# Down-projection of a two-block layer: two plain pieces ahead of the seven products, and two of the four weight sums made by accumulating transfers

## What is computed

```python
def swiglu(h, w_gate_up, w_down):
    gu = jnp.einsum('bsd,df->bsf', h, w_gate_up)
    gate, up = jnp.split(gu, [FFN_HIDDEN], axis=-1)
    return jnp.einsum('bsf,fd->bsd', jax.nn.silu(gate) * up, w_down)
...
    f = (jax.nn.gelu(g, approximate=True) * u) @ w_down[l]
```

## Time and profile before

| | |
|---|---|
| median of 3 runs | 2674.47 us |
| the profiled execution | 2673.37 us |
| its span, first to last instruction | 2671.6 us |
| TensorE busy | 2640.9 us, 99% |
| DVE, ACT, POOL busy | 1856.3, 1303.7, 3.5 us (69%, 49%, 0%) |
| mean granted clock of TensorE | 0.999 of full speed |
| HBM traffic | 497 MB, mean 186 GB/s |

### The profile page before, as it was taken

The page is one execution under the profiler, slowest core; times in us unless marked ns, Lnnn a source line. Parts: engine busy times, 40 slices in busy tenths (PEclk is TensorE's granted clock), DMA queues, the critical chain, the costliest instruction groups (busy, mean ns, idle before and its releaser), DMA issues.

```text
span 2671.6 us, 37118 instructions
## 1 busy us (share of the span) xinstructions
PE 2640.9 (99%) x13950; PEld 2272.8 (85%) x13950; DVE 1856.3 (69%) x1881; ACT 1303.7 (49%) x1313; POOL 3.5 (0%) x8
## 2 busy tenths in 40 slices
PE   9999999999999999999999999999999999999998
PEld 8888888888888888888888788888888888888877
DVE  7646666665555556875558768888777787677877
ACT  6544444444445444444445556645554454444444
POOL 0000000000000000000000000000000000000000
PEclk9999999999999999999999999999999999999999
DMA  7555555455555555555554554543555546555553
GB/s 250 189 189 174 174 187 188 173 190 190 218 191 179 189 188 206 198 204 184 189 188 162 191 194 172 178 151 133 199 173 188 188 161 217 194 188 189 186 211 134
DMA packets 71871, 497.23 MB, mean 186 GB/s; under 512 B 8183, under 2 KB 9432, under 8 KB 12648
## 3 DMA queue, kind: packets, MB, share of 16 engines
q1 hardware_dynamic: 71784, 496.06, 52.9%
HBM read 493.93 MB, written 2.10 MB: 186 GB/s over the span
## 4 chain that ended last, share of the span: by engine, by line
PE 93%; DVE 4%; ACT 1%; issue 1%; DMA 1%; DVEq 0%; SPq 0%; ACTq 0%
PE acc L2261 37%; PE acc L2269 19%; PE acc L2317 10%; PE acc L2493 7%; PE acc L2324 5%; PE acc L2498 3%; PE acc L2342 2%; DVE w_lo L1285 2%; PE acc L2338 2%; PE acc L2336 2%; PE acc L2365 1%; ACT w_hi L735 1%; PE acc L2620 1%; PE acc L2372 1%; PE aux L2761 1%
## 5 line engine op out<-in xcount | busy, mean ns | idle before, releaser
L1285 DVE TENSOR_TENSOR w_lo<-raw,w_hi 128x2048 fp32r<-128x2048 f32 (+1 forms) x467 | 1063.0, 2280 | 342.7 <-ACT w_hi L735 315.4
L735 ACT ACTIVATE w_hi<-raw 128x2048 fp32r<-128x2048 f32 (+1 forms) x467 | 889.4, 1906 | 801.6 <-PE acc L2261 337.2
L2261 PE MATMUL acc<-xa,w_hi 128*128 128x512 f32 x4480 | 1071.4, 391 | 0.2 <-ACT w_hi L735 0.2
L2261 PEld LDWEIGHTS acc<-xa,w_hi 128*128 128x128 f32 x4480 | 824.3, 188 | 161.8 <-issue 1.1
L2269 PEld LDWEIGHTS acc<-xa,w_lo 128*128 128x128 f32 x4480 | 574.1, 191 | 23.6 <-DVE w_lo L1285 2.0
L2269 PE MATMUL acc<-xa,w_lo 128*128 128x256 f32 x4480 | 581.6, 283 | 1.2 <-DVE w_lo L1285 1.2
L1297 DVE TENSOR_TENSOR tmp<-acc,small 128x512 f32<-128x512 f32 x120 | 82.9, 691 | 234.9 <-ACT small L745 234.4
L2317 PE MATMUL acc<-w_hi,hid 128*128 128x512 f32 x768 | 182.6, 390 | 0.0
L2493 PE MATMUL acc<-w_hi,xa 128*128 128x512 f32 x768 | 182.3, 390 | 0.0
L2317 PEld LDWEIGHTS acc<-w_hi,hid 128*128 128x128 f32 x768 | 143.8, 188 | 29.8
L2493 PEld LDWEIGHTS acc<-w_hi,xa 128*128 128x128 f32 x768 | 143.8, 188 | 29.7
(11 more groups left out here) (379 smaller groups left out, 2097.9 us busy)
## 6 DMA issues: line engine op xcount, KB each, us to landing
raw<-in_w_in SPq DMA_DIRECT2D x158, 1024.0 KB, 4.9
raw<-in_w_gate_up SPq DMA_DIRECT2D x88, 1024.0 KB, 4.9
raw<-in_w_down SPq DMA_DIRECT2D x88, 1024.0 KB, 4.9
raw<-in_w_up SPq DMA_DIRECT2D x87, 1024.0 KB, 4.9
raw<-in_w_out SPq DMA_DIRECT2D x32, 1024.0 KB, 4.9
raw<-in_w_uq SPq DMA_DIRECT2D x3, 1024.0 KB, 4.9
h_tok<-in_x_tok SPq DMA_DIRECT2D x1, 2048.0 KB, 9.3
raw<-in_w_ukv SPq DMA_DIRECT2D x4, 512.0 KB, 3.5
```

The costliest lines, as they stand in the source:

```text
L735: act.activation(hi_part(u, run)[:, 0:kt * P], raw_of(u)[:, 0:kt * P], ACT.Copy).then_inc(hi_made, splits(u, run))
L1285: dve.tensor_tensor(lo_part(u, run)[:, 0:kt * P], raw_of(u)[:, 0:kt * P], hi_part(u, run)[:, 0:kt * P], ALU.subtract).then_inc(lo_made, sp ...
L2261: last = pe.matmul(acc[:, bnk], w_hi[:, u % SPLIT, k * P:(k + 1) * P], x[:, k0 + k], start=first and k == 0, stop=False)
```

## The change

1. The order of a pass is now PLAIN_1, PLAIN_2, M_1, M_5, M_2, PLAIN_3, M_6, M_3, M_7, MIXED, PLAIN_4, M_4, PLAIN_5, PLAIN_6. PLAIN_2's piece is the fifth load of a pass and lies in the slot of PLAIN_1.
2. DVE makes two sums of a pass instead of four: w_sum = B_12 - B_11 as before, and at the end B_21 = B_21 - w_sum. The two between are transfers issued by POOL that add B_22, read once more from HBM, to the slot of B_12 (for M_7) and to w_sum (for M_6). The second waits for M_5's low part, which reads w_sum, and for the first transfer.
3. B_12 + B_22 takes the place of B_22 - B_12, so `hidden_sums` changes signs; it has the same instructions.
4. `weight_sum(u, 1)` moves: in the last `gated` from behind the split of the first piece to behind that of the second; between two passes from PLAIN_5 to PLAIN_6, behind the two additions of `added`.
5. Steps at the ends (squares, transposes, gains) are hung on other forms, as the old ones have moved.

```diff
-PLAIN_1, M_1, M_5, M_2, PLAIN_2, M_6, M_3, M_7, PLAIN_3, M_4, MIXED, PLAIN_4, PLAIN_5, PLAIN_6 = range(FORMS)
+PLAIN_1, PLAIN_2, M_1, M_5, M_2, PLAIN_3, M_6, M_3, M_7, MIXED, PLAIN_4, M_4, PLAIN_5, PLAIN_6 = range(FORMS)
...
     (3, ((0, 1), (1, 1), (2, 1), (3, 1))),
+    (0, ((12, 0), (13, 0), (14, 0), (15, 0))),
     (0, ((4, 0), (5, 0), (6, 0), (7, 0))),
-    (1, ((12, 0), (13, 0), (14, 0), (15, 0))),
...
-FREED_BY = (None, None, None, None, PLAIN_1, M_1, PLAIN_2, M_3, M_7, PLAIN_3, M_4)
-NEXT_SLOTS = (2, 3, 1, 0)
+FREED_BY = (None, None, None, None, PLAIN_1, PLAIN_2, M_1, PLAIN_3, M_3, M_7, M_4)
+NEXT_SLOTS = (1, 2, 3, 0)
...
                 if u in WEIGHT_SUMS:
                     act.wait_ge(w_summed, WEIGHT_SUMS[u])
+                elif u in ADDED_SUMS:
+                    act.wait_ge(w_added, ADDED_SUMS[u])
...
+            def down_sums(start, name):
+
+
+                for n, u in enumerate(s for s in PASS_STARTS if start <= s < start + GROUPS * FF_UNITS):
+                    b_22 = d[name][n // PASSES, n % PASSES, B_22]
+                    pool.wait_ge(w_summed, sums_before(u) + 1)
+                    pool.dma_start(raw[:, PIECE_RAW[u, B_12][0]], b_22, accum_op=ALU.add).then_inc(w_added, 16)
+                    pool.wait_ge(lo_made, u + M_5 + 1)
+                    pool.wait_ge(w_added, 16 * (sums_before(u) + 1))
+                    pool.dma_start(w_sum[:], b_22, accum_op=ALU.add).then_inc(w_added, 16)
+
+            down_sums(U_FF1, "w_down")
             pool.wait_ge(folded, 3)
...
                     out_, a, b = w_sum[:], piece(u, B_12), piece(u, B_11)
                 if n == 2:
-                    dve.wait_ge(lo_made, u + M_5 + 1)
-                    piece_loaded(u, B_22)
-                    out_, a, b = w_sum[:], piece(u, B_22), w_sum[:]
-                if n == 3:
-                    out_, a, b = piece(u, B_12), piece(u, B_22), piece(u, B_12)
-                if n == 4:
                     dve.wait_ge(lo_made, u + M_2 + 1)
-                    dve.wait_ge(w_summed, sums_before(u) + 2)
+                    dve.wait_ge(w_added, 16 * (sums_before(u) + 2))
                     out_, a, b = piece(u, B_21), piece(u, B_21), w_sum[:]
...
-                for m, (out_, a, b, op) in enumerate(((x_22, x_21, x_22, ALU.add), (x_21, x_11, x_21, ALU.subtract),
-                                                      (x_11, x_22, x_11, ALU.subtract), (x_12, x_12, x_11, ALU.subtract))):
+                for m, (out_, a, b, op) in enumerate(((x_22, x_21, x_22, ALU.subtract), (x_21, x_21, x_11, ALU.subtract),
+                                                      (x_11, x_11, x_22, ALU.subtract), (x_12, x_12, x_11, ALU.subtract))):
...
                             split(u + 2, run)
-                        if last and p:
-                            weight_sum(u0 + 2 * GT, 1)
                         total(t, run, 2)
                         dve.tensor_tensor(tmp[:, 0:2], tmp[:, 0:2], rstd2, ALU.mult).then_inc(gate_in, 1)
                         if p or ahead < 2:
                             split(u + 3, run)
+                        if last and p:
+                            weight_sum(u0 + 2 * GT, 1)
...
-                        if form == PLAIN_5 and p + 1 < PASSES:
+                        if form == PLAIN_6 and p + 1 < PASSES:
                             weight_sum(u + FORMS, 1)
```

More of the change, by code:

```diff
@@ L161 @@
     (3, ((0, 1), (1, 1), (2, 1), (3, 1))),
[1 row of a table added]
     (0, ((4, 0), (5, 0), (6, 0), (7, 0))),
[1 row of a table removed]
     (1, ((16, 0), (17, 0), (18, 0), (19, 0))),
[3 rows of a table removed]
[3 rows of a table added]
     (0, ((16, 1), (17, 1), (18, 1), (19, 1))),
 )
-B_11, B_22, B_12, B_21 = 1, 2, 3, 4
-PIECE_OF = {PLAIN_1: 0, M_1: B_11, M_2: B_21, M_3: B_22, PLAIN_2: 5, PLAIN_3: 6, MIXED: 7, PLAIN_4: 8, PLAIN_5: 9, PLAIN_6: 10,
+B_11, B_22, B_12, B_21 = 1, 2, 3, 5
+PIECE_OF = {PLAIN_1: 0, M_1: B_11, M_2: B_21, M_3: B_22, PLAIN_2: 4, PLAIN_3: 6, MIXED: 7, PLAIN_4: 8, PLAIN_5: 9, PLAIN_6: 10,
             M_7: B_12, M_4: B_21}
-FREED_BY = (None, None, None, None, PLAIN_1, M_1, PLAIN_2, M_3, M_7, PLAIN_3, M_4)
-NEXT_SLOTS = (2, 3, 1, 0)
+FREED_BY = (None, None, None, None, PLAIN_1, PLAIN_2, M_1, PLAIN_3, M_3, M_7, M_4)
+NEXT_SLOTS = (1, 2, 3, 0)
 def raw_places():
@@ L552, in sums_before @@
         def sums_before(u):
[L555 to L558 removed]
+            return 2 * PASS_STARTS.index(u)
+        WEIGHT_SUMS = {s + form: sums_before(s) + n for s in PASS_STARTS for form, n in ((M_5, 1), (M_4, 2))}
+        ADDED_SUMS = {s + form: 16 * (sums_before(s) + n) for s in PASS_STARTS for form, n in ((M_7, 1), (M_6, 2))}
         def next_unit(u, run):
@@ L1250, in _ @@
                             act.sem_inc(small_made, 2 * COLS)
-                        if g and p and form == PLAIN_2:
+                        if g and p and form == M_7:
                             out_square(1, 0)
@@ L2206, in _ @@
                             snap(u, b_22, M_7, ff_out[:, 2 * p, 1])
-                        if form == MIXED:
+                        if form == M_7:
+                            weight_sum(u, 2)
+                        if form == M_4:
                             if g:
@@ L2222, in _ @@
                             snap(u, b_12, M_5, ff_out[:, 2 * p + 1, 1])
-                        if form == M_2:
-                            weight_sum(u, 3)
-                        if form == M_3:
-                            weight_sum(u, 4)
-                        if form == PLAIN_5 and p + 1 < PASSES:
+                        if form == PLAIN_6 and p + 1 < PASSES:
                             weight_sum(u + FORMS, 1)
-                        if g and p and form == PLAIN_3:
+                        if g and p and form == MIXED:
                             out_gain(1, 0)
@@ L2390, in down @@
                 plain(PLAIN_1, b_11, 8, first=True)
+                plain(PLAIN_2, b_11, 12)
                 pe.wait_ge(acc_free, b_22 + 1)
@@ L2395, in down @@
                 product(u + M_2, b_11, *hidden(4, 0))
-                plain(PLAIN_2, b_11, 12)
+                plain(PLAIN_3, b_11, 16)
                 pe.wait_ge(snapped, snaps + 1)
@@ L2402, in down @@
                 product(u + M_7, b_22, *hidden(0, 1), final=True, more=True)
-                plain(PLAIN_3, b_11, 16)
-                product(u + M_4, b_21, *hidden(4, 1))
                 if p == 0:
                     pe.wait_ge(op_lo, v1 + GT)
-                pe.wait_ge(snapped, snaps + 4)
-                both_columns(u + MIXED, t)
+                both_columns(u + MIXED, t, snaps + 4)
+                if after:
+                    after(MIXED)
                 plain(PLAIN_4, b_12, 8)
+                product(u + M_4, b_21, *hidden(4, 1), final=True)
                 if not staggered:
```

61 lines of the change are left out of this document (31 added, 30 removed), and 6 rows, old and new, of the table PIECES.

## The result

The changed kernel takes 2716.27 us (median of 4 runs, 2708.99 to 2718.47), the kernel before 2674.45 in the same runs: a ratio of 1.0152, with a 95% interval of 1.0135 to 1.017. It is slower by 41.8 us. The forecast was 2705, with a range from 2672 to 2742. The profiled execution has a span of 2716.4 us, 44.8 more than before. First the page of the changed kernel: busy times, DMA queues, and issues with their median time to landing.

A forecast was written before the change was run, and what follows sets the result against it. It took TensorE's matmul stream plus holes, at most 18.7 us, to bound the kernel. The order's +5 us and the transfers' +26 us made +31 on a profiled 2673.4 us, hence 2705 us, range 2672 to 2742.

The forecast's parts named there:

- PLAIN_2 ahead of M_1: First passes: PLAIN_2's load, asked for late, delays low parts and M_1; 4.2 us in each FF1 group, 6.1 in FF2.
- Without the new transfers, +5 us: The order alone, all passes: first passes +2.6, +2.3, +1.4, -0.1; fourth pass -4.3; last pass +3.
- the second passes have nothing late: Second passes without transfers: DVE has two sums of 2.29 us fewer, so the fourth pass's 4.3 us go.
- Moving MIXED before M_4 moves one wait for a snapshot: Late in a pass: costs nothing, as DVE reaches that snapshot earlier with the sums ahead of it gone.
- L = 8.5 us: Assumed latency of each accumulating transfer by POOL, taken between 7.9 and 9.3 us; L from 6.6 to 10 had chance 0.52.
- the 7.9 by that rule: Alternative transfer latency: two moves of 3.0 us plus 1.9 us not data; the sum would be 9 us lower.
- M_6's high part late by 2L - 15.1 and by 2L - 13.2: Two chained transfers hold M_6: 1.9 us late in a first pass, 3.8 in a second, low part 0.5 more.
- The +26 us for the transfers: Waits for M_6 over the eight passes: 4 x 2.4 + 3 x 4.3 + 4.8, less 1 for overlap.
- L right but passes longer would mean that loads and additions delay one another: Sign to look for in the changed profile: passes longer than 63 to 66 us (first) and 61 to 62 (second).
- Rival 1: Accumulations are quick, up to 6.6 us, and hide in all passes: 2679 us, from 2675 to 2683; chance 0.17.
- Rival 2: Faster: PLAIN_2's late load does not reach M_1, whose first-pass wait is below 1.2 us: 2666 us; chance 0.16.
- Rival 3: Accumulations are slow, over 10 us, by slow additions or SP loads sharing the engines: +43 us, 2748 us; chance 0.15.

## Why the prediction was right, and where it was not

The sign and the size class were right: 2716 against 2705, inside the range, and slower, with 0.75. The mechanism of the larger half was not.

- **PLAIN_2 ahead of M_1** was right to 0.2 us in three of four first passes. M_1's high part was forecast 3.2 us late: gaps of 3.22, 3.24 and 3.23 us between matmuls in three first passes, 4.53 in the fourth; less a matmul's own 0.23 us, that is 3.0 and 4.3 us. PLAIN_2's low part was forecast 0.5 and 2.15 us late: gaps of 0.66, 0.68, 2.19 and 2.19, so 0.4 and 2.0. That the two plain pieces are not slack but expose a load was shown by the kernel that puts the gate function first. The 1.3 us more in the last first pass are in the trace: there ACT loads a table between its copy to `hid` and M_1's split, as it did ahead of M_5's before the change (1.28 us from 2549.46), and the forecast had no term for it:

```profile
2589.99 1.28 ACT L755 ACT_TABLE_LOAD   x1
```

- **Without the new transfers, +5 us** is mis-sized: 17 us by the kernel with all sums on DVE. That "the second passes have nothing late" failed there: each holds 2.2 to 4.8 us of lateness and slow matmuls, for PLAIN_2's load, PLAIN_3's, and `ff_out` (only the last one's, 2.8, was in the sum, as 3). The first passes, 63.8 to 66.4 us, are 1.5 to 2.8 us over the forecast too, with slow matmuls in each. "Moving MIXED before M_4 moves one wait for a snapshot", costed at nothing, looked at DVE's snapshots only. In the third group ACT makes them, and its copy `ff_out` now stands behind a split that waited 4.11 us for its load: 4.3 us of waits in the change. The turn after the first block, 3.5 us to the good, was not seen either.
- **L = 8.5 us** against 8.4 and 8.0, and of the chain 16.7 us in the first pass (1095.2 to 1111.93), so 8.35 a step. The Trainium skill's rule on the reduce primitive (Collectives: The Full Stack, "The bandwidth ceiling", on reduce-scatter) is two sources read for each write. The trace agrees: 5.6 us of the DMA engines for an addition against 2.7 for a copy; the 7.9 by that rule was as near as the 8.5. The Trainium skill's 6.15 us for a plain GpSimd load of 1 MB (DMA: Bandwidth & Descriptors, "Bandwidth") is above the 5.2 to 5.5 of the plain copies here, from issue to landing, and far below an addition's 8.0 to 8.4.
- **M_6's high part late by 2L - 15.1 and by 2L - 13.2** is the step that failed. It counted PLAIN_3 as 5.46 us of TensorE's time and never timed PLAIN_3's load, which the same text did for PLAIN_2's. That load goes into M_1's slot, and M_1's low part is now ready only 17 us into a first pass: 16.9 + 4.9 + 1.9 is 23.7, and TensorE is there at 23.5. All its slack is gone before any addition. Then the addition holds the DMA engines for 5.6 us in the same stretch. The +26 us for the transfers came out as 24, by another cause, and that the two lie so close is luck: in the change M_6 makes TensorE wait for 1.8 us in all, plain pieces for 22.7. With one addition, which TensorE never waits for, plain pieces make it wait for 22.7 us too, and for 4.6 when that addition is held.
- The prediction named the sign by which this would be known ("L right but passes longer would mean that loads and additions delay one another"), and gave it no price. The first passes took 65.9 to 67.4 us for a forecast of 63 to 66, the second 64.7 to 66.5 for 61 to 62.
- **The clock** had no term. It takes 11 us more than before in the matmuls. By the kernel with filled waits some 5 of these are time, a difference that is not clear of noise; a part of the rest covers M_6.
- Rival 1 (quick accumulations) falls with L, though the plain copies show its picture: 2690, not 2679, as the order alone costs 17. Rival 2 fails where it said that it would be decided: M_1 waits for 3 us. Rival 3 falls with L, which is not over 10; but its second condition, loads of SP that share the engines, is what came true, on the loads' side.

What stays open: the same chain's lateness was not tried alone in the change's order, with PLAIN_3's load out of the way and both additions in place. The 1.19 and 1.73 us of M_6 with filled waits are the nearest row. Nor do the runs tell how much time the low clock costs, as the gain of filled waits is not clear of noise.

## What to carry to other kernels

Time every load from the instruction that frees its slot to the instruction that wants it, in the new order, before asking what the new instructions cost: a reordering of uses moves the requests of later loads too. A transfer that nobody waits for still has a price, the DMA engines' time, and it is paid by whichever load is asked for while it runs; start it where the loads have slack (2664 us), or hold it until the tight load has landed (24 us here). Where holes are filled or shortened, look for what stands behind them: here they covered M_6's lateness.

## What the runs showed of the hardware

- An addition of 1 MB (fp32) in a transfer from HBM, issued by POOL, lands after 8.0 to 8.4 us in the median (7.8 to 9.7) and takes 5.6 us of all 16 DMA engines; the same bytes as a plain copy from the same queue 5.2 to 5.5 in the median and 2.7; a load by SP 4.9 and 3.0.
- In the change, a load asked for while one addition runs lands after 5.1 to 9.6 us, the later the more of the addition is still to come; with two additions, after up to 12.1.
- TensorE's granted clock fell from 2.4 to 1.2 GHz for 3.4 to 10.2 us at waits of 1.8 to 4.4 us, though it was 98% busy over the span. With matmuls in those waits 3.4 of 37.4 us were left. Not every such wait is followed by one: in the sixth pass TensorE stood for 3.32 us and the clock was 1.00 throughout.
